# Experts' down products in three passes from rounded parts, their weights split on ScalarE and VectorE

## The reference, cut to what matters

```python
def hier_moe(h, ...):                       # hf: 512 x 1024
    ...                                     # each token: one group of 4 experts, 2 experts in it
    for gi in range(N_GROUPS):
        sl = slice(gi * EXPERTS_PER_GROUP, (gi + 1) * EXPERTS_PER_GROUP)
        hg = jnp.einsum('td,edf->etf', hf, w_exp_gate[sl])       # 1024 -> 256
        hu = jnp.einsum('td,edf->etf', hf, w_exp_up[sl])         # 1024 -> 256
        act = jax.nn.silu(hg) * hu * combine[:, sl].T[:, :, None]
        y = y + jnp.einsum('etf,efd->td', act, w_exp_down[sl])   # 256 -> 1024
```

## Time and profile before

| what | value |
|---|---|
| time, median of 3 runs | 1854.32 us (1854.29 to 1857.3) |
| time of the profiled execution | 1852.99 us |
| its span on the core | 1851.2 us |
| PE busy | 1713.7 us, 93% |
| DVE, ACT, POOL busy | 1206.5, 478.3, 676.2 us |
| first U to the end of the span (experts) | 1567.85 to 1851.2 us |
| bytes moved | 230.54 MB |

### The profile page before, as it was taken

How to read it: one execution, slowest core, us unless ns; L and a number is a source line. 1 busy time by engine, 2 the same in 40 slices (tenths; PEclk the granted TensorE clock), 3 DMA queues, 4 the chain that set the end, 5 groups by cost and what they waited for, 6 DMA issues and landing times.

```text
span 1851.2 us, 29396 instructions
## 1 busy us (share of the span) xinstructions
PE 1713.7 (93%) x12018; PEld 1324.5 (72%) x12018; DVE 1206.5 (65%) x1611; ACT 478.3 (26%) x725; POOL 676.2 (37%) x382
## 2 busy tenths in 40 slices
PE   6999989887979999999879999998898998999998
PEld 4888667776757777777658787777676876666665
DVE  6959576654379888888677159387444525666674
ACT  3112334421121111101231122221232004444542
POOL 2765000001526666666436534345234752000000
PEclk8999789998989999999989999999898998999999
DMA  5223332120242222222222211113121253788884
GB/s 215 92 93 112 114 126 68 64 94 24 69 171 91 91 91 91 91 91 91 71 90 91 92 62 55 66 46 131 46 68 47 91 205 148 278 339 333 335 346 164
DMA packets 34070, 230.54 MB, mean 125 GB/s; under 512 B 4132, under 2 KB 4388, under 8 KB 8232
## 3 DMA queue, kind: packets, MB, share of 16 engines
q1 hardware_dynamic: 30240, 214.48, 32.0%
q10 hardware_dynamic: 2136, 10.24, 1.4%
q0 software_dynamic: 1584, 4.21, 0.7%
HBM read 220.98 MB, written 9.50 MB: 125 GB/s over the span
## 4 chain that ended last, share of the span: by engine, by line
PE 77%; DVE 13%; ACT 4%; issue 3%; DMA 3%; DVEq 0%; SPq 0%; POOL 0%; ACTq 0%; POOLq 0%
PE psum L401 76%; DVE arena L1615 4%; DVE arena L1609 3%; DMA arena<-units 2%; ACT arena L1233 2%; PE psum L405 1%; DVE arena L1612 1%; ACT L1233 1%; DVE expert_lo L1609 1%; DMA normed<-units 1%; ACT expert_hi L1233 1%; DVE residual L1609 0%; DMA arena<-x 0%; ACT tiny L1233 0%; DVE tiny L1623 0%
## 5 line engine op out<-in xcount | busy, mean ns | idle before, releaser
L1233 ACT ACTIVATE arena<-psum 128x512 f32<-128x512 f32 (+1 forms) x294 | 148.6, 520 | 876.9 <-PE psum L401 764.0
L401 PE MATMUL psum<-arena 64*64 64x64 f32 (+6 forms) x2820 | 225.6, 268 | 28.7 <-DVE arena L1609 14.5
L401 PEld LDWEIGHTS psum<-arena 64*64 64x64 f32 (+4 forms) x2820 | 153.0, 153 | 85.1 <-issue 51.2
L401 PE MATMUL psum<-normed_hi,w_in_hi 128*128 128x512 f32 x504 | 202.2, 401 | 5.7 <-DVE in_lo L1609 3.2
L401 PE MATMUL psum<-normed_hi,w_in_lo 128*128 128x512 f32 x504 | 199.2, 395 | 0.0
L1615 DVE SCALAR_TENSOR_TENSOR arena<-arena,fixed_data 128x512 f32<-128x512 f32 x134 | 190.3, 1420 | 13.5 <-DVE arena L1612 0.2
L401 PE MATMUL psum<-in_lo,w_in_hi 128*128 128x512 f32 x504 | 198.8, 395 | 0.0
L1609 DVE TENSOR_TENSOR arena<-arena,psum 128x512 f32<-128x512 f32 (+2 forms) x200 | 110.7, 588 | 118.2 <-PE psum L401 71.6
L2462 POOL TENSOR_TENSOR w_ff_lo<-weight_ring,w_ff_hi 128x1024 fp32r<-128x1024 f32 x66 | 167.1, 2533 | 5.5
L2462 POOL TENSOR_TENSOR w_in_lo<-weight_ring,w_in_hi 128x1024 fp32r<-128x1024 f32 x63 | 160.5, 2547 | 5.3
L2460 POOL TENSOR_SCALAR w_in_hi<-weight_ring 128x1024 fp32r<-128x1024 f32 x63 | 72.4, 1149 | 211.8 <-PE psum L401 201.1
(11 more groups left out here) (248 smaller groups left out, 3525.8 us busy)
## 6 DMA issues: line engine op xcount, KB each, us to landing
weight_ring<-units SPq DMA_DIRECT2D x124, 1024.0 KB, 4.8
arena<-units SPq DMA_DIRECT2D x55, 1024.0 KB, 6.9
normed<-units SPq DMA_DIRECT2D x20, 1024.0 KB, 7.4
slots<-arena ACTq DMA_DIRECT2D x7, 516.0 KB, 8.7
arena<-slots SPq DMA_DIRECT2D x7, 516.0 KB, 5.9
fixed_data<-fixed ACTq DMA_DIRECT2D x1, 2944.0 KB, 11.9
arena<-x SPq DMA_DIRECT2D x4, 512.0 KB, 5.9
arena<-bias_rows ACTq DMA_DIRECT2D x2, 896.0 KB, 5.1
```

The lines of the kernel that those rows point to most:

```text
L401: return nc.tensor.matmul(o, l, r, start=start, stop=stop)
L1233: return nc.scalar.activation(o, i, func, **kw)
```

## The change

D(s) becomes 12 matmuls of the same size in three passes from parts, hi by hi, hi by lo, lo by hi, instead of 4 in plain float32. For this:

- ScalarE: the evacuation of T(s) writes the rounded activations (`e_actt_hi`, semaphore `expert_act_hi`) and no longer frees the bank; `down_hi(s + 1)`, a rounding of 128x2048, comes behind `expert_hi(s + 2, 1)`; at i = 2 `rows_hi(b + 1)` first does the eight 128x128 operations that scale and shift the gathered rows, which were VectorE's (for block 0 it does the four of the second half).
- VectorE: behind `expert_lo(s + 2)` it takes the remainder of the activations from PSUM (`e_actt_lo`, 128x256), which frees the bank, and behind `add_rows` and `scale_of` it takes `down_lo(s + 1)`, a subtraction of 128x2048 in place; `split_rows` keeps only its two subtractions.
- TensorE's D(s) waits for `down_split`, not for the load.
- The rounded down weights lie over constants and matrices that are no longer used and in the second ring slot; `x_scale` moves from there to the constants of `bucket`.

```diff
@@ buffers
-        x_scale = [ring[:, 1, i * P:(i + 1) * P] for i in range(2)]
+        x_scale = [C("bucket", a=i * P, b=(i + 1) * P) for i in range(2)]
+        e_down_lo = [part(f"down_lo{i}", o, UNIT, b)[:, :] for i, (o, b) in
+                     enumerate(((8192, arena_at), (8192 + UNIT, arena_at), (0, ring_base)))]
+        e_down_hi = [part(f"down_hi{i}", o, UNIT, b)[:, :] for i, (o, b) in
+                     enumerate(((C0 + CONSTS["level0t"][0], fix_at), ((M0 + 7) // 8 * 8, fix_at), (UNIT, ring_base)))]
@@ TensorE, expert_down
-                pe.wait_ge(sem(f"expert_down{s % 3}_loaded"), 16 * (s // 3 + 1))
-                w = e_down[s % 3].rearrange("p (h k c) -> p h k c", h=2, k=2)
+                pe.wait_ge(sem("down_split"), s + 1)
+                hi, lo = [w[s % 3].rearrange("p (h k c) -> p h k c", h=2, k=2) for w in (e_down_hi, e_down_lo)]
                     for k in range(2):
-                        last = mm(o, e_actt[s % 2][:, k * P:(k + 1) * P], w[:, h, k, :], i == 0 and k == 0, i == 3 and k == 1)
+                        c = slice(k * P, (k + 1) * P)
+                        mm(o, e_actt_hi[s % 2][:, c], hi[:, h, k, :], i == 0 and k == 0, False)
+                        mm(o, e_actt_hi[s % 2][:, c], lo[:, h, k, :], False, False)
+                        last = mm(o, e_actt_lo[s % 2][:, c], hi[:, h, k, :], False, i == 3 and k == 1)
@@ ScalarE
+            def down_hi(s):
+                if s < NX:
+                    act.wait_ge(sem(f"expert_down{s % 3}_loaded"), 16 * (s // 3 + 1))
+                    f(e_down_hi[s % 3], e_down[s % 3], ACT.Copy).then_inc(sem("down_hi"), 1)
             def rows_hi(b):
+                for i in range(2):
+                    if b or i:
+                        filled(act, "rows", 2 * b + i)
+                        for k in range(4 * i, 4 * i + 4):
+                            last = f(xt_raw[xt_of(b)][:, k * P:(k + 1) * P], PSB[4 + i][:, k % 4 * P:(k % 4 + 1) * P],
+                                     ACT.Identity, scale=gm2[:, k:k + 1], bias=mod[:, 24 + k:25 + k])
+                        last.then_inc(freed("rows", 2 * b + i), 1)
@@ ScalarE, slot s (down_hi(0) stands ahead of the loop)
-                evac("expert_act", s, e_actt[s % 2], PSB[bank_of("expert_act", s)][:, 0:256])
+                filled(act, "expert_act", s)
+                f(e_actt_hi[s % 2], PSB[bank_of("expert_act", s)][:, 0:256], ACT.Copy).then_inc(sem("expert_act_hi"), 1)
                 expert_hi(s + 2, 1)
+                down_hi(s + 1)
                 if i == 2 and b + 1 < NB:
                     rows_hi(b + 1)
@@ VectorE, slot s (down_lo(0) stands behind expert_lo(1))
+            def down_lo(s):
+                if s < NX:
+                    dve.wait_ge(sem("down_hi"), s + 1)
+                    tt(e_down_lo[s % 3], e_down[s % 3], e_down_hi[s % 3].bitcast(F32), ALU.subtract)\
+                        .then_inc(sem("down_split"), 1)
                 if s + 2 < NX:
                     expert_lo(s + 2)
+                dve.wait_ge(sem("expert_act_hi"), s + 1)
+                tt(e_actt_lo[s % 2], PSB[bank_of("expert_act", s)][:, 0:256], e_actt_hi[s % 2].bitcast(F32), ALU.subtract)\
+                    .then_inc(freed("expert_act", s), 1)
                 if i == 0 and b:
                     add_rows(b - 1)
                 if i == 0 and b + 1 < NB:
                     scale_of(b + 1)
+                down_lo(s + 1)
                 if i == 2 and b + 1 < NB:
                     split_rows(b + 1)
```

More of the change, by code:

```diff
@@ L330, in xt_of @@
             return 1 + b % 2 if b else 0
-        x_scale = [ring[:, 1, i * P:(i + 1) * P] for i in range(2)]
+        x_scale = [C("bucket", a=i * P, b=(i + 1) * P) for i in range(2)]
         xb = [A(22528 + ROW * i, ROW) for i in range(3)]
         y_tmp = A(16384)
-        e_sg, e_act, e_actt = [[A(16896 + 512 * j + 256 * i, 256) for i in range(2)] for j in range(3)]
+        e_sg, e_act = [[A(16896 + 512 * j + 256 * i, 256) for i in range(2)] for j in range(2)]
+        e_actt_hi, e_actt_lo = [[part(f"act_{what}{i}", 16896 + 512 * j + 256 * i, 256)[:, :] for i in range(2)]
+                                for what, j in (("hi", 2), ("lo", 1))]
         gt2_row = tiny[:, :]
@@ L1588, in _ @@
             rows_hi(0)
+            down_hi(0)
             for s in range(NX):
@@ L2380, in split_rows @@
             def split_rows(b):
[L2382 to L2385, removed]
+                if b == 0:
+                    filled(dve, "rows", 0)
+                    for k in range(4):
+                        last = ts(xt_raw[0][:, k * P:(k + 1) * P], PSB[4][:, k * P:(k + 1) * P],
                                   gm2[:, k:k + 1], mod[:, 24 + k:25 + k], ALU.mult, ALU.add)
-                    last.then_inc(freed("rows", 2 * b + i), 1)
+                    last.then_inc(freed("rows", 0), 1)
                 for i in range(2):
@@ L2418, in _ @@
             expert_lo(1)
+            down_lo(0)
             dve.wait_ge(sem("rows0_loaded"), 16)
```

## The result

The changed kernel takes 1859.9 us, median of 19 runs (1855.29 to 1866.97), against 1854.52 us for the kernel before (19 runs). The ratio is 1.0029, 95% interval 1.0019 to 1.0039: 5.4 us slower, a little more than the 0.2% that can be told apart. The time forecast was 1855.3 us, in the range of 1845 to 1864; "same" was the likeliest of the three outcomes, and "slower" is what came.

The account below looks back on a forecast made before the run. PE set the time, but the chain of waits through four queues was to decide: 0.4 + 1.8 + 0.4 - 1.65 = +0.95 us on 1854.32 gave 1855.3 us, range 1845 to 1864.

Parts of the forecast that it names:

- signs named: D about 2.8 us, PE waiting on DVE's activations, DVE near 90% busy, PE about 92%, blocks of 40 to 41 us.
- TensorE's saving of 0.63 us per D: On TensorE, each D shorter by about 0.63 us, 28 of them by 17.6 us if nothing else were late.
- The chain: Next T waits for second expert_lo, activation remainder, down_lo and activations on DVE: 7.25 us after the second weight rounding starts.
- the step with add_rows: T(12) to T(13): add_rows and scale_of, 2.97 us, join the waits on DVE; 11.2 us instead of 10.70.
- The third step: T(11) to T(12): a late transfer, then the waits through DVE, set it; 9.45 us instead of 9.20.
- H(11): Start of slot 11's second rounding of weights on ScalarE, ended by a transfer, forecast at T(10) + 11.5 us.
- The scaling on ScalarE: Eight scalings of rows moved from DVE to ACT, taken at 0.3 us each, 2.4 us for eight.
- The rival in which these decide: ScalarE's moved scalings, at 0.46 us each, make T(10) to T(11) 10.6 us; 1862 to 1865 us, chance 0.2.
- From one block to all: Four blocks from T(5): 161.2 against 159.4 us, +1.8; last block +0.4; T(5) later by 0.4 us.
- The start: U(0) some 0.5 us later from moved scalings and down_lo(0); first slots give back about as much.
- TensorE's clock as a rival: Between D(12) and T(13), about 2 us of PE idleness lowers the clock; 1864 us, chance 0.1.
- The partial gain as a rival: TensorE's gain comes through in part if scalings cost 0.2 us and transfers land early; about 1845 us, chance 0.2.

Follow-up runs that it names:

- SyncE's edit: Gate and up units of slot s + 1 issued ahead of slot s's down unit; on the kernel before: 1849.06 us, ratio 0.9967.
- the first order and the last: Changed kernel as first built, 1859.9 us; same operations with queues reordered, rows split at i = 2, gate and up loads issued earlier, 1837.2 us.
- the reordered loads: Changed kernel with only SyncE's queue edited, gate and up units of slot s + 1 ahead of slot s's down unit: 1860.0 us, ratio 1.0031.

## Why the prediction was right, and where it was off

The time is in the range and the new chain is there, but the point is 4.6 us too low, where a rise of only 0.95 us was forecast, and "same" was put at 0.40 against 0.37 for "slower". The range held since it was drawn wide enough for the slower rivals, not since the sum was that good. Of the signs named, the block of 40 to 41 us came (40.57); from 1650 to 1800 us DVE was busy 84%, not near 90, and PE 90%, not 92.

- *TensorE's saving of 0.63 us per D.* Right: 10.41 instead of 11.04 us where PE sets the step.
- *The chain.* Right for two of the steps and nearly in its sizes: for the block that was worked out, 10.4, 9.3, 9.45 and 11.2 us were forecast, sum 40.3, and 10.41, 9.50, 9.39 and 10.88 measured, sum 40.18. Moving down_lo out of it took the step with add_rows to 8.9 us, which shows the cause there. The third step came out right by another way than forecast, which is luck: T(12) was to wait for the activations, 7.25 us after H(11), but it is D(11) that waits for act_lo and puts T(12) 7.54 us after H(11) at 1689.44. That wait stood in no term. And the step with add_rows was forecast 0.3 us too long, as H(12) came with the end of T(12), not with a transfer.
- *The scaling on ScalarE.* Forecast 0.3 us a step, measured 0.341; it made the step with rows 9.50 and not 9.3 us. The rival in which these decide had its point at 0.35 us and just didn't happen.
- *From one block to all.* Here is most of the miss. The four blocks between T(5) and T(21) took 162.5 us, not 161.2, as one held a transfer late enough for a step of 10.97 us (T(16) at 1738.68). The last block took 40.30 and not 39.2: its third step fell to 8.64 us without rows among its transfers, but the step with add_rows took 11.73 instead of 10.9, as the second rounding was held by its transfer until 1.7 us after T(24), not 0.7. The block to T(5) took 40.32 us, 1.0 more than forecast, with 11.75 us at the first add_rows for the same reason. The term "late transfers", read from one block and assumed mild elsewhere, was too small by some 3.4 us. ScalarE's first rounding ahead of T(16) and second rounding ahead of T(25):

```profile
1728.67 1.92 ACT L1242 ACTIVATE expert_hi<-arena 128x2048 fp32r<-128x2048 f32 x1 [1.95 <-DMA arena<-units]
...
1820.20 1.92 ACT L1242 ACTIVATE expert_hi<-arena 128x2048 fp32r<-128x2048 f32 x1 [0.27 <-DMA arena<-units]
```

- *The start.* T(1) is 1.65 us later than before, forecast about 0.1. Most of it is not the change: the first products of rows begin at 1557.18 here and at 1555.00 before, ahead of any moved work, and the start of U(0) lies anywhere from 1567.0 to 1573.0 us in the 14 profiled executions. U(0) begins 3.4 us after the second half of the rows was there (ScalarE's first scaling at 1566.22), against 2.8 before; this 0.6 us is the change's, forecast 0.5. PE's timeline:

```profile
1557.18 6.00 PE L407 MATMUL psum<-arena 128*128 128x128 f32 x37 [3.97 <-DVE arena L1637]
...
1569.63 0.50 PE L407 MATMUL psum<-expert_hi,rows_hi 128*128 128x512 f32 x1 [3.44 <-DVE rows_lo L1634]
```

- *The end.* T(25) to the end: 27.2 against 28.6 us, 1.4 saved, 1.65 forecast.
- *The sum.* +0.95 us were forecast and +6.2 came between the two profiled executions. The 5.2 us that were missing are 1.55 at the start, 1.0 to T(5), 1.3 in four blocks, 1.1 in the last and 0.25 at the end.
- *TensorE's clock as a rival, chance 0.1.* It was not seen in the profiled execution of the changed kernel, but it was real: gaps of the forecast size do lower the clock in some executions. Over the 19 runs, the time rises by 1.4 us for each 0.001 by which the mean clock is lower (1.0 us over 23 of the kernel before), and the mean is 0.0011 lower than the 0.9600 of those 23. So 1 to 1.5 of the 5.4 us go with the clock. That is a relation between runs; the share was not separated by an experiment.
- *The partial gain as a rival, chance 0.2.* It did not happen with this order, and it did with another: 10.2 of the 17.6 us without SyncE's edit, and 10 to 12 us where both kernels have it (1837.2 against 1849.06, ratios 0.9912 and 0.9967). Its ground, that PE has nearly all of the time, was true; the objection, that transfers end two of the waits, was worth 6 us of the some 22 between the first order and the last.

What stays open: how the 16 to 20 us of added work divide between down_hi, act_lo and down_lo, as they were only moved and not taken out one by one; and what decides whether a gap of some 2 us lowers the clock.

## What to carry to other kernels

When work is moved from the busiest engine to idle ones, the shares don't say whether it is free; its place in their queues does. An operation that is needed a slot later must not stand ahead of one that the busiest engine waits for now, and a bound that a step hides today (here the transfers) must be priced in every period, not in one. After such a move, order the queues by due time before judging it: here the same operations gave 1859.9 us in one order and 1843.3 in another, and 1837.2 with the gate and up weights issued earlier too.

## What the runs showed of the hardware

A wait of TensorE of 1.85 us was enough for the granted clock to fall to 0.50 (window from 1665 us of the reordered loads), while the same wait at T(5) of that execution left it at 1.00, and so did waits up to 1.87 us in the changed kernel. Each such fall at rows_in cost 1.6 us on top of the wait. ScalarE needs 0.34 us in step for a 128x128 scaling from PSUM with a scale and a bias per partition, 475 ns long each, where VectorE's step for the same is 0.32 us (2.55 us for eight).
